# Out-projection of a hybrid decoder step, emitted inside the second FFN in that FFN's tile order and by output half, with input items of the FFN prepared between its tiles

## The reference, cut to what matters

```
x1 = LN1(alpha*x  + 0.5*SwiGLU_a(x))
x2 = LN2(alpha*x1 + [MLA(x1) ; RWKV7(x1)] @ w_out)      # w_out is 1024 x 1024
y  = LN3(alpha*x2 + 0.5*SwiGLU_b(x2))
```

## Time and profile before

| | |
|---|---|
| runs of the kernel before | 2457.91, 2441.76, 2458.9 us (median 2457.91) |
| profiled execution, its time | 2459.68 us |
| its span | 2458.0 us |
| PE busy | 2371.1 us, 96% of the span |
| DVE, ACT, POOL busy | 1567.6, 1012.3, 432.8 us |
| mean granted PE clock | 0.986 of 2.4 GHz |

### The profile page before, as it was taken

The page is one execution under the profiler, slowest core; times in us unless marked ns, Lnnn a source line. Parts: engine busy times, 40 slices in busy tenths (PEclk is TensorE's granted clock), DMA queues, the critical chain, the costliest instruction groups (busy, mean ns, idle before and its releaser), DMA issues.

```text
span 2458.0 us, 52723 instructions
## 1 busy us (share of the span) xinstructions
PE 2371.1 (96%) x21093; PEld 2101.3 (85%) x21093; DVE 1567.6 (64%) x2730; ACT 1012.3 (41%) x1786; POOL 432.8 (18%) x421
## 2 busy tenths in 40 slices
PE   8999999999999999999999999999799999999997
PEld 7999999988878799666657988877799999998886
DVE  6777766565685847677633444463777776666568
ACT  5333333354545646433333333342533333345343
POOL 4232100000042212000000122333522210000005
PEclk8999999999999999999999999999899999999999
DMA  4465523397554444422122022244355552339653
GB/s 159 163 204 173 199 82 113 113 316 231 177 186 134 136 114 118 134 58 61 33 70 101 28 73 66 72 164 138 128 197 195 175 187 83 110 129 316 214 174 116
DMA packets 306657, 346.59 MB, mean 141 GB/s; under 512 B 39633, under 2 KB 206370, under 8 KB 304882
## 3 DMA queue, kind: packets, MB, share of 16 engines
q1 hardware_dynamic: 252946, 286.85, 36.2%
q10 hardware_dynamic: 52256, 53.62, 6.2%
q0 software_dynamic: 1216, 2.80, 0.4%
HBM read 244.25 MB, written 98.41 MB: 139 GB/s over the span
## 4 chain that ended last, share of the span: by engine, by line
PE 83%; DVE 8%; issue 4%; ACT 3%; POOL 1%; DMA 1%; SPq 0%; ACTq 0%; POOLq 0%; DVEq 0%
PE ps_b L763 18%; PE ps_a L763 17%; PE ps_a L473 6%; PE ps_b L473 6%; PE ps_rk L3077 6%; PE ps_pj L1525 4%; PE ps_wo L3872 4%; PE ps_mp L2265 3%; PE ps_mp L2291 2%; PE ps_pj L1507 2%; PE ps_mp L2279 1%; PE ps_rk L3167 1%; PE ps_mp L2250 1%; DVE W_a L1061 1%; PE ps_rk L3073 1%
## 5 line engine op out<-in xcount | busy, mean ns | idle before, releaser
L763 PE MATMUL ps_b<-X_b,W_b 128*128 128x272 f32 x3696 | 466.3, 289 | 4.5 <-DVE X_b L1022 3.9
L763 PEld LDWEIGHTS ps_b<-X_b,W_b 128*128 128x128 f32 x3696 | 464.9, 189 | 5.9 <-DVE X_b L1022 4.1
L763 PE MATMUL ps_a<-X_a,W_a 128*128 128x272 f32 x3696 | 465.4, 288 | 4.5 <-DVE X_a L1022 1.7
L763 PEld LDWEIGHTS ps_a<-X_a,W_a 128*128 128x128 f32 x3696 | 463.5, 189 | 6.4 <-DVE G_a L1079 3.0
L473 PE MATMUL ps_a<-W_a,H_a 128*128 128x512 f32 x924 | 216.1, 390 | 0.0
L473 PE MATMUL ps_b<-W_b,H_b 128*128 128x512 f32 x924 | 214.8, 389 | 1.0 <-DVE H_b L1108 1.0
L473 PEld LDWEIGHTS ps_b<-W_b,H_b 128*128 128x128 f32 x924 | 173.3, 188 | 37.3 <-DVE W_b L1061 1.4
L473 PEld LDWEIGHTS ps_a<-W_a,H_a 128*128 128x128 f32 x924 | 173.8, 188 | 36.0
L844 ACT ACTIVATE W_a<-wraw_a 128x512 fp32r<-128x512 f32 x154 | 95.8, 629 | 163.7 <-PE ps_a L763 65.1
L844 ACT ACTIVATE W_b<-wraw_b 128x512 fp32r<-128x512 f32 x154 | 95.8, 629 | 162.7 <-PE ps_b L763 64.4
L1061 DVE TENSOR_TENSOR W_b<-wraw_b,W_b 128x512 fp32r<-128x512 f32 x154 | 113.7, 744 | 69.4 <-ACT W_b L844 69.4
(11 more groups left out here) (495 smaller groups left out, 4290.7 us busy)
## 6 DMA issues: line engine op xcount, KB each, us to landing
hraw_a<-hidden SPq DMA_DIRECT2D x77, 256.0 KB, 3.6
hraw_b<-hidden SPq DMA_DIRECT2D x77, 256.0 KB, 3.7
wraw_pj<-in_w_in SPq DMA_DIRECT2D x28, 512.0 KB, 3.7
wraw_a<-in_ffa_w_gate SPq DMA_DIRECT2D x22, 512.0 KB, 4.7
wraw_a<-in_ffa_w_up SPq DMA_DIRECT2D x22, 512.0 KB, 4.9
hraw_a<-in_ffa_w_down SPq DMA_DIRECT2D x22, 512.0 KB, 5.4
down_sums<-hraw_a SPq DMA_DIRECT2D x11, 1024.0 KB, 6.5
wraw_a<-down_sums SPq DMA_DIRECT2D x44, 256.0 KB, 2.9
```

What stands on the lines that cost most here:

```text
L763: last = nc.tensor.matmul(ps[:, bank + p, :PIECE], W[:, n % WC, wp, k * P:(k + 1) * P], operand(i, xp)[:, k, p * PIECE:(p + 1) * PIECE], s ...
```

## The change

**Where it is emitted.** The out-projection is no block of its own. It returns an object whose parts (`sync`, `tensor`, `scalar`, `vector`, `pool`) the second FFN calls at the head of its own engine lists, so that both can be mixed.

**Order and halves.** Its tiles go in `X_ORDER`. From the second tile on PE does output half 0 (24 matmuls) and then half 1. All tiles after the first put their output into the same two banks, and all rows are turned in one pair of banks; a half waits until DVE has taken the previous tile's half out. PE waits for a tile's own low part before it turns the next.

**Items between tiles.** In the middle of tiles 2 to 7 (by place) PE turns one row of the FFN's input (`turn_x(n-2)`), six of nine. `x_parts(0)` and `x_parts(1)` are placed between the halves of tiles 3 and 5 on DVE (ahead of `y_high` 5 and 7 on ACT). `x_parts(2)` comes after the last tile, with the root, inverse, scale and gain of the last row threaded through it. Items 3 and 4 follow as before.

**Rows.** `RowNorm` works by halves: sum and statistics for each half. The gain multiply of a row follows its own scale, with `y_low` of two tiles on ahead of it. Memory is laid out anew, and so the first row's two halves wait for `y_made` of groups 8 and 9 (`values_read`), and DVE's `w_low(4)` waits until the states have landed in DRAM (`states_landed`). SP sends the states ahead of blocks 5 to 7 of `w_out`, and the gains and the third tile's rows wait for the last `w_split`.

**Pieces.** In both FFNs a slot's columns are cut 256 and 288 (`LEFT`, `RIGHT`) in place of 272 and 272, so that the second FFN's operands of the right half lie apart.

The core of the diff:

```diff
-HALF, PIECE = 544, 272
+HALF, LEFT, RIGHT = 544, 256, 288
@@ up_slot
-                            last = nc.tensor.matmul(ps[:, bank + p, :PIECE], W[:, n % WC, wp, k * P:(k + 1) * P],
-                                                    operand(i, xp)[:, k, p * PIECE:(p + 1) * PIECE],
+                            last = nc.tensor.matmul(ps[:, bank, 512 - LEFT:] if p == 0 else ps[:, bank + 1, :RIGHT],
+                                                    W[:, n % WC, wp, k * P:(k + 1) * P], operand(i, xp, p)[:, k, :],
@@ ffn, PE
+            if before is not None:
+                before.tensor(pe, turn)
+                before.banks_free(pe)
+            for k in range(0 if before is None else 6, NT):
                 turn(k)
@@ ffn, SP
+                before.sync(sp, load_x)
+                load_w(0)
+                load_x(6)
+                load_x(7)
+                before.weights_read(sp)
+                load_w(1)
+                before.last_row(sp)
+                load_x(8)
@@ out_projection, SP
+            before.store_states(sp)
+            before.products(sp)
             for k in range(WS, KD):
                 load_w(k)
-            before.store_states(sp)
-            before.products(sp)
-            sp.wait_ge(S.w_split.h, S.w_split.at(WS))
+            for n in range(NT):
+                norm.load_rows(sp, n)
+                if n == 0:
+                    sp.wait_ge(R["w_split"].h, R["w_split"].at(KD))
+                    norm.load_gains(sp)
+                if n >= 2:
+                    norm.store(sp, n - 2)
+                if n + 2 < NT:
+                    rows_in(n + 2)
...
+                if 2 <= n < NT - 1:
+                    load_x(n - 2)
@@ out_projection, PE
+            for n in range(NT):
+                pe.wait_ge(R["ylo"].h, R["ylo"].at(n + 1))
+                if 3 <= n < NT - 1:
+                    turn(n + 1)
...
+                for step in range(2 * KD):
+                    c, k = (step % 2, step // 2) if n == 0 else divmod(step, KD)
+                    if n >= 2 and k == 0:
+                        pe.wait_ge(N.z_made.h, N.z_made.at(2 * (n - 1) + c + 1))
...
+                    if k == KD - 1 and c == 0 and 2 <= n < NT - 1:
+                        turn_x(n - 2)
@@ out_projection, DVE
+            for k in range(2, 4):
+                w_low(k)
+            before.states_landed(dve)
+            for k in range(4, 6):
+                w_low(k)
             before.norm_dve(dve, chain, NGR - 2)
...
+            for n in range(NT):
+                norm.half(dve, chain, n, 0)
+                if n in (3, 5):
+                    x_parts(n // 2 - 1)
+                norm.half(dve, chain, n, 1)
+                norm.variance(dve, n)
+                if n < NT - 1:
+                    norm.inverse(dve, chain, n)
+                if n + 2 < NT:
+                    y_low(n + 2)
+                if n < NT - 1:
+                    norm.gain(dve, n)
+            x_parts(2, lambda: norm.inverse(dve, chain, NT - 1), lambda: norm.gain(dve, NT - 1))
```

More of the change, by code:

```diff
@@ L825, in _ @@
             pe.wait_ge(S.const_ready.h, S.const_ready.at(1))
-            for k in range(NT):
-                if before is not None and k in (0, 2):
-                    before.free(pe, k // 2)
+            if before is not None:
+                before.tensor(pe, turn)
+                before.banks_free(pe)
+            for k in range(0 if before is None else 6, NT):
                 turn(k)
@@ L867, in fill @@
                     wait_weight_slot(act, n - WC)
-                elif before is not None and n >= 1:
-                    before.ended(act)
+                if before is not None and n in (WC - 2, WC - 1):
+                    act.wait_ge(Q.slo_made.h, Q.slo_made.at(4 * 4))
                 copy(W[:, n % WC, 0, :], source(n)).then_inc(Q.w_hi.h, 1)
@@ L939, in scale_res @@
                 nc.scalar.activation(z_of(t), z_of(t), ACT.Copy, scale=2 * ALPHA).then_inc(Q.res_scaled.h, 1)
-            for j in range(5):
+            if before is not None:
+                before.scalar(act, x_parts)
+            for j in range(0 if before is None else 3, 5):
                 if j == 4:
@@ L1027, in x_parts @@
                 low_part(6, a22)
+                if first is not None:
+                    first()
                 dve.wait_ge(made.h, made.at(4 * j + 1))
@@ L1032, in x_parts @@
                 low_part(0, a11)
+                if second is not None:
+                    second()
                 dve.wait_ge(made.h, made.at(4 * j + 2))
@@ L1125, in token_sum @@
                 V.tensor_tensor(z, z, ps[:TS, bank, :], ALU.add).then_inc(Q.z_made.h, 1)
-            for j in range(5):
+            if before is not None:
+                before.vector(dve, chain, x_parts)
+            for j in range(0 if before is None else 3, 5):
                 if j == 4:
@@ new lines, in out_projection, with raw, w_high_at, w_low_at @@
+    w_in = [Sem(nc, sems, f"wo_w_in{u}") for u in range(WS)]
+    y_in = [Sem(nc, sems, f"wo_y_in{u}") for u in range(2)]
+    N = LnSems(nc, sems)
+    def raw(k):
+        return wraw[:, k % WS * D:(k % WS + 1) * D]
+    def w_high_at(k):
+        return whi[:, k, :]
+    def w_low_at(k):
+        return wlo[1][:, (k + 1) % 3, :] if k < 3 else wlo[0][:, k - 3, :]
+    def out_bank(n):
+        return 0 if n == 0 else 6
+    def half_sum(dve, n, c, z, x):
+        dve.wait_ge(R["m_done"].h, R["m_done"].at(2 * n + c + 1))
+        if n == 0:
+            before.values_read(dve, NGR - 2 + c)
+        return nc.vector.scalar_tensor_tensor(z, x, ALPHA, ps[:rows_of(tiles[n]), out_bank(n) + c, :], ALU.mult, ALU.add)
@@ new lines, in sync, with weights_read, last_row, row_stored @@
+            norm.store(sp, NT - 2)
+        def weights_read(self, sp):
+            sp.wait_ge(R["m_done"].h, R["m_done"].at(2 * NT))
+        def last_row(self, sp):
+            norm.store(sp, NT - 1)
+        def row_stored(self, sp, n):
+            norm.wait_stored(sp, n)
+        def tensor(self, pe, turn_x):
+            def turn(n):
+                r, s = rows_of(tiles[n]), n % 2
+                pe.wait_ge(y_in[s].h, y_in[s].at(32 * (n // 2 + 1)))
+                if n == 0:
+                    before.keys_read(pe)
+                if n >= 1:
+                    pe.wait_ge(R["ylo"].h, R["ylo"].at(n))
@@ L3891, in w_high, with scalar, y_high, norm_rows @@
+        def scalar(self, act, x_parts):
+            def y_high(n):
+                r, s = rows_of(tiles[n]), n % 2
+                act.wait_ge(R["y_turned"].h, R["y_turned"].at(n + 1))
+                if n >= 2:
+                    act.wait_ge(R["m_done"].h, R["m_done"].at(2 * (n - 1)))
+                nc.scalar.activation(yhi[:, s, :, :r], turned(n), ACT.Copy).then_inc(R["yhi"].h, 1)
             def w_high(k):
                 act.wait_ge(w_in[k % WS].h, w_in[k % WS].at(16 * (k // WS + 1)))
-                nc.scalar.activation(whi[:, k, :], raw(k), ACT.Copy).then_inc(S.w_hi.h, 1)
+                nc.scalar.activation(w_high_at(k), raw(k), ACT.Copy).then_inc(R["w_hi"].h, 1)
+            def norm_rows(n):
+                norm.root(act, n)
+                norm.scale(act, n)
```

519 lines of the change are left out of this document (245 added, 274 removed).

## The result

| | before | after |
|---|---|---|
| median of runs | 2456.32 us (2441.76 to 2460.53, 19 runs) | 2465.83 us (2457.22 to 2472.39, 19 runs) |
| ratio, 95% interval | | 1.0045 [1.0033, 1.0057] |
| span of the profiled execution | 2458.0 us | 2460.7 us |
| last states' copy to the end of gating, group 9 | 25.6 | 30.6 |
| ... to the last projection matmul | 109.8 | 126.1 |

The change costs 0.45%, 11 us by the ratio and 9.5 by the two medians; forecast were 7.8. The two profiled spans differ by 2.7 only, because the mixer, which the change doesn't touch, took 10 us less in the one of after (1096.7 us from the first FFN's last slot to the last states' copy, 1107.1 before); over all kernels of this study it lay from 1092.7 to 1109.2. So I don't compare ends of spans, but distances from one instruction that all kernels have: DVE's copy of the last states.

What follows compares the result with a forecast made beforehand. PE, busy 96%, was taken as the bound, with a 31.4 us gap before the second FFN to win from. Terms 18.3 − 9.0 − 1.5 = +7.8 on 2457.9 gave 2465.7 us, range 2447 to 2480.

Steps and rivals of the forecast that it cites:

- The pieces at nothing: FFN slots: cutting columns 256 and 288 instead of 272 twice changes the time by 0.
- Rival (b): FFN slots: weight load is the limit from 272 columns down, +27 us, 2492 with the seam; chance 0.08.
- y of group 9 late by 4: Head of the projection: states sent before blocks 5 to 7 delay `y_made` of group 9 from 1631.3 to 1635.3.
- Row 0's chain of 16.1: Head: from group 9's gating, row 0 takes 16.1 us until turned, so the third tile ends 13.9 us later.
- rival (a): Head is cheap: group 9 not late, rows back faster, tail 20; −0.5 us, or −5 giving 2452; chance 0.15.
- Tiles of 13.0: Out-projection after the third tile: each tile takes 13.0 us.
- Waits hidden in tiles 3 to 8: Out-projection: row returns, `x_parts`, low parts and bank waits are hidden; only five more turns cost, 4.4 us.
- Rival (c): Head: rows 0 and 1 both late and clock falls in PE's waits, +8 us more, 2474 to 2480; chance 0.10.
- The tail of 22.4: Last projection matmul to first slot: last row's norm, DRAM way and turns take 22.4 us for 31.4, −9.0.
- 1.5 back from the slow start: Start of second FFN's slots: PE comes straight from identity turns, so the slow clock's 1.5 us is won back.
- The seam: Out-projection and tail up to the second FFN's first slot: 18.3 later, less 9.0, so +9.3 us.
- Rival (d): Change does what it is called after: tiles undelayed, tail near 17, head hidden; −12 us, 2446; chance 0.07.

Runs made afterwards that it cites:

- b_pieces: The kernel before with only the pieces of a slot changed to 256 and 288 columns, in both FFNs; ratio to before 0.9993.
- a_noitems: The kernel after with no items between tiles: FFN rows loaded, turned and split behind the last tile; ratio to before 1.0086.
- a_values: The kernel after with the first two rows in their own buffers, so only the third waits for `values_read`; ratio to before 1.0021.
- a_states: The kernel after with group 8's norm ahead of the wait for the states, on DVE and ACT; ratio to before 1.0030.
- a_y32: The kernel after with the projection's row tiles and the buffers behind them moved 32 bytes, off a multiple of 64; one run, 2467.23 us.
- a_272: The kernel after with pieces of 272 and the old place of the operands in the first FFN; ratio to before 1.0031.
- a_ident: The kernel after with 56 identity turns ahead of the last row's turn in place of 28 behind it; ratio to before 1.0033.

## Why the prediction was right

The forecast was 2465.7 and the range 2447 to 2480; the median is 2465.83. In the ratio the change costs 11 us and not 7.8, so that the two agree to 0.1 us is luck: the runs of before came out 1.6 us lower than the three that I started from, and some of the terms below are off in opposite directions. The mechanism held: a late gating of group 9, row 0's chain behind it, and a tail set by the last row's way through DRAM.

- **The pieces at nothing.** Held, by b_pieces (ratio 0.9993). Rival (b) is out.
- **y of group 9 late by 4.** 5.0. I had group 8's root behind ACT's copy of block 7 (+3.5; it was +4.4), and DVE "about as late". Both held: ACT's copy ends 0.47 us before the root starts, and in the end the root waited for DVE's statistics, behind the states and block 5. The 2.5 us to start and land, in the sum for block 7, came from no row.
- **Row 0's chain of 16.1.** 14.6, from POOL's gating to `turn_x(0)`: the load took 3.45 and not 4.8, since the earlier trace rows has its price from loads of residual rows sent together with others. The 0.6 for gain against POOL was 0.5. Too short by 1.0 there and too long by 1.5 here nearly cancel, and the third tile ended at 1657.4 on before's clock (forecast 1657.9): +13.4 for +13.9. That this chain alone makes the 13.4 I had not asked; a_noitems has 11.0 of them without it, from PE's other waits.
- **That POOL's order holds row 0 up in any case,** the argument against rival (a), is what a_values showed. It and a_states give back a third of the loss each.
- **Tiles of 13.0.** 12.67, the term furthest from its reasons: 2 us over six tiles, from where the operands lie (a_y32). I took before's pace over unasked.
- **Waits hidden in tiles 3 to 8.** Held: no wait of PE there. Rival (c) had the clock fall in PE's waits; it did, to 0.50 in the third tile, but cost only time that PE would have waited for row 0. Its +8 on top is out.
- **The tail of 22.4.** 24.1 along the chain (23.9 by the marks): norm 10.4 (10.3), the way through DRAM 6.7 (6.6), turn 1.11, and the identity 5.95 where I carried over 4.39. I had put "turns at full clock" in the range as a gain; they ran at half clock throughout, behind a longer idle time than before's.
- **1.5 back from the slow start.** Seen (clock 1.00 from the first slot), but B is 0.7 longer, not 1.5 shorter: PE waits 1.6 us for `G_b` sums in it where it waited 0.5.
- **The seam.** +8.7 at the first slot for +9.3 forecast. The rest of the 11 us doesn't lie there; in this trace the first FFN's slots are 3.5 us longer, of which the prediction knew nothing.
- **Rival (d),** that it does what it is called after, fails on the head alone: with four edits there it comes true in part, at 139.7 for before's 141.3.

**What stays open.** The first FFN's slots, long ahead of the seam, take 467.9 to 471.4 us in the nine kernels built on the kernel after (469.3 on average) and 467.1 to 468.7 in the five built on before (467.7 on average), one trace each. PE is idle there, mostly for DVE, 7.7 us in after and 4.3 in before, but also 6.1 in b_pieces, whose slots took 467.5. The ranges overlap, so most of after's 3.5 us may be scatter between executions; some 1.6 us may be real. In b_pieces the pieces alone don't bring it, and a_272, with the first FFN's pieces and operands as they were, has 469.4, neither before's nor after's. The cause was not found.

## What to carry to other kernels

Work that is moved ahead of a barrier is worth what it takes out of the barrier's stretch less what it adds ahead of it (here 7.6 us less in the tail, for 5.2 us of turns and their waits among the tiles), and memory and queue order that make room for it add their own waits at the other end: list these (`values_read`, the states ahead of the weights, the gains ahead of the rows) and look for who already fixes the time of each, since one of them alone gives back only a third. When a row has to be normed and go through DRAM and back, its chain (14.6 us here) is the length to plan the slack for, and the last one of them bounds the seam however early the others are. And compare two kernels by marks from a common instruction, where an untouched stretch of 1100 us varies by 16 from one execution to the next.

## What the runs showed of the hardware

- Matmuls of 512 columns came every 227.5 ns at full clock in the kernel after, and every 233 ns with the row tiles and the buffers behind them 32 bytes further on (a_y32).
- Pieces of 256 and 288 columns cost together what two of 272 do: slots of 466.6 us with either (b_pieces, before).
- A gain on POOL that starts with DVE's takes 1.80 us for 1.30, DVE's nothing more. The other way, DVE's first low part of a weight block (of two SBUF operands) took 4.15 us while POOL worked on sums, the same form 0.69 eleven us later:

```profile
1737.89 4.15 DVE L1107 TENSOR_TENSOR W_b<-wraw_b,W_b 128x512 fp32r<-128x512 f32 x1 [0.69 <-ACT W_b L880]
...
1749.05 0.69 DVE L1107 TENSOR_TENSOR W_b<-wraw_b,W_b 128x512 fp32r<-128x512 f32 x1
```

- In a_ident 3.3 us of idle PE, a row's turn of 0.71 us and 2.1 of idle, all behind 56 turns of the identity, were followed by a clock of 0.50. In after a single wait of 3.3 us in the third tile was followed by a clock of 0.50 from 1636 to 1639, and in a_values one of 3.29 us by 0.50 from 1654 to 1656.
